# Expert weights loaded ahead of the stage, and token rows gathered in fp32 straight from x

## The chip, the cores and the metric

One core of a Trainium2 chip runs the whole program. The time is that of the device in microseconds (us), from one launch; the kernel before took 2052.31 us (median of 3 runs, 2049.75 to 2055.69). A core has five engines with queues of their own: TensorE (PE in the profile, with its weight loads as PEld), VectorE (DVE), ScalarE (ACT), GpSimd (POOL) and SyncE (SP), which here issues the DMAs. Between them stand semaphores, written out by hand in this kernel.

## The reference, cut to what matters

The program is a stack of layers on 256 tokens of 1024 numbers: a mixer, a mixture of experts, a gated embedding, a spatial gating mixer, an RWKV mixer and two FFNs. The change touches the mixture of experts and what stands before it:

```python
hn = _rmsnorm(x, g_ffn_norm)                   # [256, 1024]
logits = hn @ w_router + b_router              # 32 experts
top_vals, top_idx = lax.top_k(logits, 4)
gates = jax.nn.softmax(top_vals, axis=-1)
...
# for each expert e, for the tokens that chose it:
hgu = xb @ w_up_gate[e] + b_up_gate[e]         # 1024 -> 2048
x_glu = jnp.minimum(hgu[:, :1024], 7.0)
x_lin = jnp.clip(hgu[:, 1024:], -7.0, 7.0)
hact = x_glu * jax.nn.sigmoid(1.702 * x_glu) * (x_lin + 1.0)
ys = hact @ w_down[e] + b_down[e]              # 1024 -> 1024
# x + sum over the four experts of ys * gate
```

All weights are fp32. One expert has 8 MB of up and gate weights and 4 MB of down weights.

## The kernel before, in words

Seven stages follow each other (line 2828), with a barrier and a clearing of semaphores between them (`end_stage`, line 117). Two matter here.

**The mixer** (line 272). Its DMA queue on SP loads seven segments of `w_in` and two halves of `w_out` into the two buffers of `raw`, each as soon as the split of the segment before into high and low parts has left its buffer (lines 379 to 386). Its work buffers (`w_part`, `x_part`, `qkT`, `soft`, `positive`, `weight`, `rope`) lie beside each other. It ends with the projection by `w_out` on PE and four additions to x (line 891).

**The expert stage** (line 895), in two blocks with a barrier between them. The first block (line 969) has the router. SP issues nine small tables, then the first up load of expert 0, the up biases, and the other five loads of expert 0 into a ring of six buffers of 2 MB, four for up and two for down. DVE sums the squares of x and makes a diagonal of 1/rms; PE turns x by it (line 168), ACT and DVE copy it to `xT` with the norm's gain, and PE makes the logits (line 267, by the helper `matmuls`). Beside this ACT writes the scaled x in another order of columns (line 1036), and ACT and DVE split it into three bf16 `parts` (lines 1040, 1066, 1042, 1098). DVE then finds the top four, the gates and who was chosen; PE counts the rank of each token in its expert (lines 1009 to 1015); DVE and PE write a list of items, one for each expert and each further 64 tokens of it. Here there are 32 items.

The second block (line 1150) is the loop over items. Each item works on up to 64 tokens:

- `pick` (DVE, line 1279) marks in a 128x64 matrix which token goes to which slot, from `rank`; `gather` (PE, line 1180) multiplies the three bf16 parts by it, 48 pieces, into bank TURN; DVE multiplies by the gain into `xsT` (line 1284).
- 32 up matmuls of 512 columns (line 1214), in fp32 (the trace shows each fp32 matmul as two pieces), two buffer quarters at a time; each used buffer is released to SP through `up_used`. The biases come by four bf16 matmuls (line 1221) from `bias_part`, and the last of them releases the fourth buffer.
- The sum of the item before is added to x's four banks (line 1194), the slots' spread is turned (line 1230), the next item's `gather` runs, `act_h` is turned (line 1238, read with a step of four numbers), ACT copies it to `hT`, and 16 down matmuls follow (line 1250). They release `down_used`.

PE does this in this order, and SP reloads a buffer as soon as it is released, in the order up 0 to 3, down 0, down 1. POOL splits the biases into bf16 parts once (lines 1166 to 1176), beside the first item; PE waits for it before the first bias matmul.

The slots' gather in one place of code:

```python
1183  for k in range(KC):
1184      out = c.banks[:, TURN, k * CAP:(k + 1) * CAP]
1185      ins = matmuls(nc, out,
1186                    [parts[:, a, tc, k * P:(k + 1) * P] for tc in range(TC) for a in range(3)],
1187                    [pick[:, tc, :] for tc in range(TC) for a in range(3)])
```

## Time and profile before

| | us |
|---|---|
| median of 3 runs | 2052.31 |
| lowest and highest | 2049.75, 2055.69 |
| the profiled execution | 2056.73 |
| its span, first to last instruction | 2055.0 |
| PE busy in the span | 1804.6 (88%) |
| DVE, ACT, POOL busy | 770.2, 520.7, 212.3 |
| DMA's share of 16 engines | 66.6% |

The profile is of one execution. "Busy" counts the time in which an engine has an instruction in work; fp32 matmuls overlap, so PE's busy time is not time at its peak. In the timeline a row is a run of equal instructions: start in us from the span's start, busy us, engine, line, operation, out<-in, count, and in brackets how long the engine stood idle before and what released it. "PEclk" is the granted clock of TensorE, 1.00 at 2.4 GHz and 0.50 at 1.2 GHz; its mean over the span is 0.953.

### The profile page before, as it was taken

The page shows a single profiled execution, that of the slowest core. Times are in us where ns is not written, and L with a number is a line of the kernel's source. Part 1 is how long each engine was busy: PE and PEld are TensorE (multiplying, and loading weights), DVE is VectorE, ACT ScalarE, POOL GpSimd, SP SyncE. Part 2 cuts the span into 40 slices and gives each one's busy share as a digit, 9 for nine tenths or more (in the row PEclk, how much of TensorE's full clock was granted, in tenths as well). Part 3 has the DMA queues.
Part 4 walks back from the last instruction along what each step waited for, and adds up shares of the span by engine and source line. Part 5 has one row for each costly group of instructions (what it writes and reads, how often), then busy time and mean ns, then how long its engine had stood idle before and what let it go on. Part 6 is the DMA issues. An engine that isn't in the chain of part 4 may idle for free. (4 is left out here: it accounts for less than half of the span.)

```text
span 2055.0 us, 28922 instructions
## 1 busy us (share of the span) xinstructions
PE 1804.6 (88%) x11506; PEld 1113.2 (54%) x11506; DVE 770.2 (37%) x1364; ACT 520.7 (25%) x804; POOL 212.3 (10%) x149
## 2 busy tenths in 40 slices
PE   6887599998989898989988889798998998888997
PEld 5664233333333333333333368777997776847996
DVE  7923411111111111111111263836555647436555
ACT  4511111110111011101110235425442303215442
POOL 3511400000000000000000034320000103300000
PEclk9999799999999999999999989998999999988998
DMA  7312799999999999999999655329441431118530
GB/s 260 135 42 79 333 409 428 428 428 426 429 428 428 428 427 427 428 428 428 427 426 428 290 199 189 144 84 326 163 163 38 173 103 51 75 28 300 187 140 31
DMA packets 104399, 554.11 MB, mean 270 GB/s; under 512 B 17377, under 2 KB 27618, under 8 KB 78898
## 3 DMA queue, kind: packets, MB, share of 16 engines
q1 hardware_dynamic: 104338, 553.26, 66.6%
q8 instruction: 42, 0.69, 0.1%
q14 instruction: 19, 0.16, 0.0%
HBM read 551.15 MB, written 2.10 MB: 269 GB/s over the span
## 5 line engine op out<-in xcount | busy, mean ns | idle before, releaser
L1214 PE MATMUL banks<-ring,xsT 128*64 128x512 f32 x2048 | 458.0, 597 | 41.9 <-DMA ring<-in_w_up 41.0
L1214 PEld LDWEIGHTS banks<-ring,xsT 128*64 128x64 f32 x2048 | 143.2, 137 | 350.7 <-issue 266.5
L1313 DVE TENSOR_SCALAR glu<-banks 128x512 f32<-128x512 f32 x32 | 22.1, 692 | 663.2 <-PE banks L1221 663.2
L1250 PE MATMUL banks<-ring,hT 128*64 128x512 f32 x1024 | 230.2, 603 | 22.0 <-ACT hT L1269 22.0
L1858 PE MATMUL banks<-f_xT_hi,f_w_hi 128*128 128x256 f32 x512 | 146.7, 287 | 21.2 <-issue 21.2
L1250 PEld LDWEIGHTS banks<-ring,hT 128*64 128x64 f32 x1024 | 71.5, 138 | 158.6 <-issue 130.5
L1858 PE MATMUL banks<-f_xT_hi,f_w_lo 128*128 128x256 f32 x512 | 146.6, 286 | 0.0
L1858 PE MATMUL banks<-f_xT_lo,f_w_hi 128*128 128x256 f32 x512 | 146.6, 286 | 0.0
L1265 ACT ACTIVATE sig<-glu 128x512 f32<-128x512 f32 x32 | 20.1, 629 | 478.2 <-DVE glu L1313 478.2
L267 PE MATMUL banks<-w_arena 128*128 128x256 f32 (+1 forms) x400 | 120.1, 462 | 5.9 <-ACT w_arena L2649 3.6
L1858 PEld LDWEIGHTS banks<-f_xT_hi,f_w_hi 128*128 128x128 f32 x512 | 100.1, 195 | 24.4 <-issue 22.6
L1360 POOL TENSOR_TENSOR p_w_lo<-p_w_raw,p_w_hi 128x1024 fp32r<-128x1024 f32 x4 | 12.4, 3111 | 929.6 <-ACT p_w_hi L1404 929.5
L267 PEld LDWEIGHTS banks<-w_arena 128*128 128x128 f32 x400 | 77.5, 195 | 46.6 <-issue 32.3
L1858 PEld LDWEIGHTS banks<-f_xT_lo,f_w_hi 128*128 128x128 f32 x512 | 100.0, 195 | 1.8
L1858 PEld LDWEIGHTS banks<-f_xT_hi,f_w_lo 128*128 128x128 f32 x512 | 99.9, 195 | 0.0
L1943 DVE TENSOR_TENSOR f_w_lo<-ring,f_w_hi 128x1024 fp32r<-128x1024 f32 x64 | 78.2, 1224 | 28.8 <-ACT f_w_hi L1895 28.7
L1948 DVE TENSOR_TENSOR f_w_lo<-ring,f_w_hi 128x1024 fp32r<-128x1024 f32 x64 | 76.4, 1220 | 25.3 <-ACT f_w_hi L1900 25.3
L1868 PE MATMUL banks<-f_w_hi,f_h_hi 128*128 128x512 f32 x256 | 79.5, 392 | 0.0
L1868 PE MATMUL banks<-f_w_lo,f_h_hi 128*128 128x512 f32 x256 | 79.2, 390 | 0.0
L1868 PE MATMUL banks<-f_w_hi,f_h_lo 128*128 128x512 f32 x256 | 79.0, 390 | 0.0
L1271 ACT ACTIVATE e_y<-banks 128x512 f32<-128x512 f32 x32 | 19.1, 597 | 233.4 <-PE banks L1250 233.4
L1900 ACT ACTIVATE f_w_hi<-ring 128x1024 fp32r<-128x1024 f32 x64 | 66.8, 1052 | 31.6 <-PE banks L1868 23.2
(411 smaller groups left out, 2766.5 us busy)
## 6 DMA issues: line engine op xcount, KB each, us to landing
ring<-in_w_up SPq DMA_DIRECT2D x128, 2048.0 KB, 24.8
ring<-in_w_down SPq DMA_DIRECT2D x64, 2048.0 KB, 20.4
ring<-in_ffn_w SPq DMA_DIRECT2D x30, 2048.0 KB, 9.0
m_raw<-in_w_in SPq DMA_DIRECT2D x7, 2048.0 KB, 8.2
ring<-in_sgu_in SPq DMA_DIRECT2D x7, 2048.0 KB, 8.8
w_arena<-in_w_rkv SPq DMA_DIRECT2D x6, 2048.0 KB, 12.9
ring<-in_sgu_out SPq DMA_DIRECT2D x4, 2048.0 KB, 7.5
m_raw<-in_w_out SPq DMA_DIRECT2D x2, 2048.0 KB, 7.8
```

The costliest lines, as they stand in the source:

```text
L267: ins = nc.tensor.matmul(out, lhs[i], rhs[i], start=start and i == 0, stop=stop and i == n - 1)
L1214: ins = nc.tensor.matmul(c.banks[CAP * h:CAP * (h + 1), bank, :], xsT[:, k, :], up_slot[k // 2][:, o:o + BANK], start=k == 0, stop=False)
L1250: ins = nc.tensor.matmul(c.banks[CAP * h:CAP * (h + 1), DOWN, :], hT[:, at:at + CAP], down_slot[half][:, o:o + BANK], start=k == 0, stop=k ...
L1265: nc.scalar.activation(sig[:, :], glu[:, :], ACT.Sigmoid, scale=ALPHA).then_inc(sig_ready, 1)
L1271: nc.scalar.activation(y[:, :], c.banks[:, DOWN, :], ACT.Copy).then_inc(y_ready, 1)
L1313: v.tensor_scalar(glu[:, :], c.banks[:, GLU, :], LIMIT, None, ALU.min).then_inc(glu_ready, 1)
L1360: vec.tensor_tensor(w_part[1][:, k, :], w_raw[:, k, :], w_part[0][:, k, :], ALU.subtract).then_inc(w_low[k % 2], 1)
L1858: ins = nc.tensor.matmul(c.banks[:, j, 0:T], w[:, j, k, :], x[:, k, :], start=k == 0 and n == 0, stop=k == KC - 1 and n == 2)
L1868: ins = nc.tensor.matmul(c.banks[:, OUT + 2 * tc + o, :], h[:, j, tc * P:(tc + 1) * P], w[:, j, o * BANK:(o + 1) * BANK], start=False, sto ...
L1900: nc.scalar.activation(w2_hi[:, j, :], w2_raw[s][:, j, :], ACT.Copy).then_inc(w2_high, 1)
L1943: vec.tensor_tensor(w1_lo[:, j, :, :], w1_raw[s][:, :, j * P:(j + 1) * P], w1_hi[:, j, :, :], ALU.subtract).then_inc(w1_low, 1)
L1948: vec.tensor_tensor(w2_lo[:, j, :], w2_raw[s][:, j, :], w2_hi[:, j, :], ALU.subtract).then_inc(w2_low, 1)
```

## The change

Six buffers `front` of 2 MB take the place of the ring and are opened before the mixer's other buffers. The mixer's `w_part` and `x_part` lie at the same addresses (buffers 0 to 2), and `qkT`, `soft`, `positive` and `rope` are views of buffers 3 to 5; `weight` shares the memory of `scored`. At the end of the mixer's DMA queue SP loads the expert stage's nine tables, then expert 0's six loads, each after a wait for the last use of the mixer's data there. The expert stage becomes one block. The router works on x turned without a scale; the norm's gain is multiplied into `w_router` by POOL, and 1/rms comes in at the logits. The bf16 `parts` are gone: `gather` reads x itself in fp32, with a step of eight numbers, and `pick` holds 1/rms instead of 1. Ranks count from 1. Item 0 stands ahead of the loop; the list is finished and the gates are turned between its up matmuls, and the four opening matmuls of the sums come after its bias matmuls. POOL's bias split waits for `xs_ready`. At the end each of the four sums signals by itself. In the diff, the new `load_expert_tables` issues the tables as lines 972 to 982 did, and new DVE code for top four and gates, with the same operations on both halves of the tokens at once, is left out.

```diff
+UPS, DOWNS, SLOT = 4, 2, 4096
+FRONT = UPS + DOWNS
+UP_SLOT, DOWN_SLOT = (5, 4, 0, 1), (2, 3)
+LIST = 192
...
+        self.front = sb("front", [P, FRONT * SLOT])
...
+    def slot(self, i):
+        return self.front[:, i * SLOT:(i + 1) * SLOT]
+    def load_up(self, sp, e, q):
+        sp.dma_start(self.slot(UP_SLOT[q]), self.dram["w_up"][bass.ds(e * P, P), q * SLOT:(q + 1) * SLOT]).then_inc(
+            self.up_in[q], 16)
+    def load_down(self, sp, e, h):
+        sp.dma_start(self.slot(DOWN_SLOT[h]), self.dram["w_down"][bass.ds(e * (2 * P) + h * P, P), :]).then_inc(
+            self.down_in[h], 16)
...
+    with ExitStack() as under:
+        w_part = [under.enter_context(nc.sbuf_tensor(f"m_w_{n}", [P, KC, BANK], F32R)) for n in ("hi", "lo")]
+        x_part = [under.enter_context(nc.sbuf_tensor(f"m_x_{n}", [P, KC, T], F32R)) for n in ("hi", "lo")]
+    c.open_experts()
...
-        qkT = sb("qkT", [P, 4, PAIRS, T])
+        qkT = c.slot(3).rearrange("p (a i t) -> p a i t", a=4, i=PAIRS)
         decay = sb("decay", [P, HEADS, DIAG])
-        soft = sb("soft", [P, HEADS, DIAG])
-        positive = sb("positive", [P, HEADS, DIAG])
-        weight = sb("weight", [P, 2, 2, DIAG])
-        rope = sb("rope", [P, 4, TC, HEADS, HD // 2])
+        soft, positive = (c.slot(i)[:, 0:HEADS * DIAG].rearrange("p (h n) -> p h n", h=HEADS) for i in (4, 5))
+        rope = [c.slot(4 + i // 2)[:, HEADS * DIAG + i % 2 * BANK:HEADS * DIAG + (i % 2 + 1) * BANK].rearrange(
+            "p (c h d) -> p c h d", c=TC, h=HEADS) for i in range(4)]
...
+        weight = scored
...
+                c.load_expert_tables(sp)
+                sp.wait_ge(soft_done, PAIRS)
+                sp.wait_ge(roped, 2)
+                c.load_up(sp, 0, 0)
+                sp.wait_ge(arg_done, PAIRS)
+                c.load_up(sp, 0, 1)
+                sp.wait_ge(w_used, SEGS * KC)
+                c.load_up(sp, 0, 2)
+                c.load_up(sp, 0, 3)
+                c.load_down(sp, 0, 0)
+                sp.wait_ge(s_done, PAIRS)
+                c.load_down(sp, 0, 1)
...
-                for tc in range(TC):
-                    nc.scalar.activation(xn[:, tc, :].rearrange("t (k p) -> t k p", k=KC),
-                                         c.x[:, tc, :].rearrange("t (p k) -> t k p", k=KC), ACT.Copy,
-                                         scale=c.stat[:, tc:tc + 1]).then_inc(xn_ready, 1)
-                act.wait_ge(xn_ready, TC)
-                nc.scalar.activation(parts[:, 0, :, :], xn[:, :, :], ACT.Copy).then_inc(split_act, 1)
-                act.wait_ge(split_dve, 1)
-                nc.scalar.activation(parts[:, 1, :, :], xn[:, :, :], ACT.Copy).then_inc(split_act, 1)
...
+                def item(i, e):
                     for q in range(UPS):
                         sp.wait_ge(up_used, i * UPS + (q + 1 - UPS))
-                        load_up(sp, e, q)
+                        c.load_up(sp, e, q)
                     for h in range(DOWNS):
                         sp.wait_ge(down_used, i * DOWNS + (h + 1 - DOWNS))
-                        load_down(sp, e, h)
+                        c.load_down(sp, e, h)
+                sp.dma_start(chooser[:, :], c.dram["chooser"]).then_inc(bias_in, 16)
+                for i in range(3):
+                    sp.dma_start(bias[i * E:(i + 1) * E, :], c.dram["b_up"]).then_inc(bias_in, 16)
+                item(1, 1)
+                items = count(sp)
+                with sp.Fori(2, items) as i:
+                    item(i, listed_at(sp, i + EXPERT_AT, E - 1))
...
+                pool.wait_ge(c.router_in, 32)
+                nc.gpsimd.tensor_tensor(c.w_router[:, :, :], c.w_router[:, :, :],
+                                        c.col("g_ffn", 0, KC).unsqueeze(2).to_broadcast([P, KC, E]),
+                                        ALU.mult).then_inc(router_gained, 1)
+                pool.drain()
+                nc.gpsimd.memset(ones[:, :], 1.0).then_inc(ones_done, 1)
+                pool.drain()
+                for lo in (E, CAP + E):
+                    nc.gpsimd.memset(y[lo:lo + E, :], 0.0)
+                    pool.drain()
+                    nc.gpsimd.memset(spreadT[lo:lo + E, :], 0.0)
+                    pool.drain()
+                nc.gpsimd.memset(nothing[:, :], 0.0).then_inc(cleared, 1)
+                pool.drain()
                 pool.wait_ge(bias_in, 64)
+                pool.wait_ge(xs_ready, 1)
...
-                        ins = matmuls(nc, out,
-                                      [parts[:, a, tc, k * P:(k + 1) * P] for tc in range(TC) for a in range(3)],
-                                      [pick[:, tc, :] for tc in range(TC) for a in range(3)])
+                        ins = matmuls(nc, out, [c.x[:, tc, k:D:KC] for tc in range(TC)],
+                                      [pick[:, tc, :] for tc in range(TC)])
...
+                            if stop:
+                                ins.then_inc(summed, 1)
...
+                def open_sums():
+                    pe.wait_ge(cleared, 1)
+                    pe.wait_ge(list_done, 1)
+                    pe.wait_ge(gates_taken, 1)
+                    for i in range(2 * TC):
+                        nc.tensor.matmul(c.banks[:, SUM + i, :], nothing[:, 0:P], nothing[:, :], start=True, stop=False)
+                    pe.wait_ge(c.b_down_in, 32)
...
+                        if first and k == 3:
+                            finish_list()
+                        if first and k == 5:
+                            turn_gates()
...
+                    if first:
+                        open_sums()
...
+                for k in range(KC):
+                    for tc in range(TC):
+                        at = (k % 2) * T + tc * P
+                        ins = nc.tensor.transpose(c.banks[:, TURN_X + k // 2, at:at + P], c.x[:, tc, k * P:(k + 1) * P],
+                                                  c.ident[:, :])
+                    if k % 2:
+                        ins.then_inc(turned, 1)
+                pe.wait_ge(router_gained, 1)
+                for k in range(KC):
+                    pe.wait_ge(by_act, k // 2 + 1)
+                    for tc in range(TC):
+                        ins = nc.tensor.matmul(c.banks[:, LOGIT, tc * E:(tc + 1) * E], c.xT[:, k, tc * P:(tc + 1) * P],
+                                               c.w_router[:, k, :], start=k == 0 and tc == 0, stop=k == KC - 1,
+                                               skip_group_check=True)
+                ins.then_inc(routed, 1)
+                pe.wait_ge(c.r_const_in, 64)
+                pe.wait_ge(ones_done, 1)
+                pe.wait_ge(marked, 1)
+                for tc in range(TC):
+                    out = c.banks[:, RANK, tc * E:(tc + 1) * E]
+                    if tc:
+                        nc.tensor.matmul(out, ones[:, :], chosen[:, 0, 0, :], start=True, stop=False)
+                    ins = nc.tensor.matmul(out, c.upto[:, :], chosen[:, tc, 0, :], start=not tc, stop=True)
+                ins.then_inc(ranked, 1)
+                for tc in range(TC):
+                    ins = nc.tensor.matmul(c.banks[0:E3, EXTRA, 0:1], chosen[:, tc, :, :].rearrange("p b e -> p (b e)"),
+                                           ones[:, 0:1], start=tc == 0, stop=tc == 1)
+                ins.then_inc(ranked, 1)
+                gather(0)
+                pe.wait_ge(flagged, 1)
+                nc.tensor.matmul(c.banks[0:E3, EXTRA, 1:2], c.upto[0:E3, 0:E3], flag[:, :], start=True,
+                                 stop=True).then_inc(placed, 1)
+                item(0, True)
+                items = count(pe)
+                with pe.Fori(1, items) as i:
+                    item(i, False)
...
+                nc.scalar.activation(squares[:, 1, :], c.x[:, 1, :], ACT.Square, accum_out=c.stat[:, 1:2]).then_inc(
+                    squared, 1)
+                for b in range(KC // 2):
+                    act.wait_ge(turned, b + 1)
+                    nc.scalar.activation(c.xT[:, 2 * b:2 * b + 2, :].rearrange("p k t -> p (k t)"),
+                                         c.banks[:, TURN_X + b, :], ACT.Copy).then_inc(by_act, 1)
+                act.wait_ge(negated, 1)
+                for tc in range(TC):
+                    nc.scalar.activation(gate[:, tc, :], top[:, tc, 0:TOPK], ACT.Exp, bias=neg_max[:, tc:tc + 1],
+                                         accum_out=gate_sum[:, tc:tc + 1]).then_inc(exped, 1)
+                act.wait_ge(gates_taken, 1)
...
-                                              rank[:, tc, bass.ds(e, 1)], None, ALU.is_equal)
+                                              rank[:, tc, bass.ds(e, 1)], rstd[:, tc:tc + 1], ALU.is_equal,
+                                              ALU.mult)
...
+                v.nop().then_inc(halves_read, 1)
+                chain(dve, v.tensor_tensor_reduce(squares[:, 0, :], c.x[:, 0, :], c.x[:, 0, :], 1.0, 0.0, ALU.mult,
+                                                  ALU.add, c.stat[:, 0:1]))
+                dve.wait_ge(squared, 1)
+                c.dve_rstd(dve, v.tensor_scalar(rstd, rstd, 1.0 / D, EPS, ALU.mult, ALU.add), rstd)
+                dve.wait_ge(c.router_in, 32)
+                dve.wait_ge(c.r_const_in, 64)
+                dve.wait_ge(routed, 1)
...
+                dve.wait_ge(ranked, 1)
+                chain(dve, v.tensor_tensor(rank[:, :, :], c.banks[:, RANK, 0:TC * E].rearrange("p (c e) -> p c e", c=TC),
+                                           chosen[:, :, 0, :], ALU.mult))
+                pick_item(0, 0)
+                dve.wait_ge(ranked, 2)
+                v.tensor_tensor(flag[:, :], c.banks[0:E3, EXTRA, 0:1], c.extra_col[0:E3, 0:1], ALU.is_gt).then_inc(
+                    flagged, 1)
+                dve.wait_ge(bias_in, 64)
+                choose_item(0)
+                dve.wait_ge(gathered, 1)
+                take_gathered()
...
+                item(0, 0, 0, (1, 0), True)
...
+                        dve.wait_ge(summed, 2 * tc + h + 1)
```

## Rows read from the trace of the kernel before

**Rows 1.** The page's slices: GB/s in 40 equal parts of the span.

```profile
GB/s 260 135 42 79 333 409 428 428 428 426 429 428 428 428 427 427 428 428 428 427 426 428 290 199 189 144 84 326 163 163 38 173 103 51 75 28 300 187 140 31
```

**Rows 2.** Windows, mid-loop: PE, PEld, DVE, ACT, POOL busy; PEclk; DMA share; GB/s.

```profile
400.00:1000.00 600.00, 535.02 (x3296) 200.58 (x3294) 89.67 (x200) 71.49 (x102) 0.00 (x0) 1.00 1.01 428
```

**Rows 3.** Timeline, PE, items 1 and 2: start, us, operation, [idle before].

```profile
263.44 13.90 PE L1214 MATMUL banks<-ring,xsT 128*64 128x512 f32 x64
...
279.91 1.56 PE L267 MATMUL banks<-pick,parts 128*128 128x64 bf16 x48
282.35 0.72 PE L1238 MATMUL banks<-ident,act_h 128*128 128x128 f32 x4 [0.88 <-DVE xsT L1284]
283.75 7.09 PE L1250 MATMUL banks<-ring,hT 128*64 128x512 f32 x32 [0.69 <-ACT hT L1269]
290.67 13.90 PE L1214 MATMUL banks<-ring,xsT 128*64 128x512 f32 x64
```

**Rows 4.** Timeline, DVE, late in the loop: `glu` of two items.

```profile
1120.40 0.69 DVE L1313 TENSOR_SCALAR glu<-banks 128x512 f32<-128x512 f32 x1 [21.41 <-PE banks L1221]
...
1149.82 0.69 DVE L1313 TENSOR_SCALAR glu<-banks 128x512 f32<-128x512 f32 x1 [21.36 <-PE banks L1221]
```

**Rows 5.** Timeline, end of the mixer, head of the expert stage.

```profile
153.29 0.39 PE L396 MATMUL banks<-m_w_lo,m_x_hi 128*128 128x512 f32 x1
...
165.31 0.60 ACT L726 ACTIVATE xT<-banks 128x512 f32<-128x512 f32 x1 [9.05 <-PE banks L546]
...
189.88 1.23 DVE L153 CUSTOM_DVE_ANT_0 e_xn<-x 128x1024 f32<-128x1024 f32 x1 [1.15 <-PEq L120]
...
194.03 0.36 SPq L964 DMA_DIRECT2D ring<-in_w_up  x1
...
202.29 3.73 PE L267 MATMUL banks<-w_router_sb,xT 128*128 128x32 f32 x32 [1.02 <-issue]
...
210.10 0.18 DVE L1075 FIND_INDEX8 top_i<-top,logits 128x8 uint32<-128x32 f32 x1
```

**Rows 6.** Timeline, item 0: up matmuls, bias split on POOL, bias matmuls.

```profile
225.12 1.88 POOL L1166 CAST bias_part<-bias 32x2048 bf16<-32x2048 f32 x1 [32.37 <-POOLq L969]
...
232.69 16.25 PE L1214 MATMUL banks<-ring,xsT 128*64 128x512 f32 x64 [0.87 <-DVE xsT L1284]
...
247.86 1.88 POOL L1174 CAST bias_part<-bias 32x2048 bf16<-32x2048 f32 x1
...
249.93 0.62 PE L1221 MATMUL banks<-bias_part,choose 96*64 96x512 bf16 x4 [1.00 <-POOLq L1175]
```

**Rows 7.** Timeline, last item and end of the stage.

```profile
1162.88 0.60 ACT L1271 ACTIVATE e_y<-banks 128x512 f32<-128x512 f32 x1 [7.19 <-PE banks L1250]
...
1163.53 1.99 PE L1194 MATMUL banks<-e_y,spreadT 64*128 64x512 f32 x8 [0.70 <-ACT e_y L1271]
...
1165.57 2.48 DVE L1329 TENSOR_TENSOR x<-x,banks 128x512 f32<-128x512 f32 x4 [11.38 <-PE banks L1194]
```

**Rows 8.** Single lines: ns min/median/max, first and last start.

```profile
L407 PEld LDWEIGHTS banks<-ident,m_qk x16: 138/140/143, 57.5 to 59.2; 128*128 128x128 f32 x16
L1238 PEld LDWEIGHTS banks<-ident,act_h x128: 195/213/223, 255.1 to 1154.7; 128*128 128x128 f32 x128
L1238 PE MATMUL banks<-ident,act_h x128: 285/286/359, 255.1 to 1154.8; 128*128 128x128 f32 x128
L267 PE MATMUL banks<-w_router_sb,xT x32: 268/276/276, 202.3 to 205.7; 128*128 128x32 f32 x32
L1036 ACT ACTIVATE e_xn<-x,stat x2: 2149/2150/2150, 201.2 to 203.2; 128x1024 f32<-128x1024 f32 x2
L1404 ACT ACTIVATE p_w_hi<-p_w_raw x8: 1042/1050/1063, 1177.1 to 1185.7; 128x1024 fp32r<-128x1024 f32 x8
```

**Rows 9.** Timeline and windows: a clock drop; the clock after the router.

```profile
626.20 8.78 PE L1250 MATMUL banks<-ring,hT 128*64 128x512 f32 x32 [0.69 <-ACT hT L1269]
...
206.60:210.00 3.40, 0.00 (x0) 0.00 (x0) 2.62 (x4) 1.04 (x2) 0.00 (x0) 0.50 0.97 405
```

More of the change, by code:

```diff
@@ L1290, in choose_item, with item @@
                         chosen_ready, 1)
[L1292 to L1302 removed]
+                def item(i, e, b, after, first):
+                    if not first:
+                        dve.wait_ge(spread_turned, i)
                     for tc in range(TC):
@@ new lines, in _ @@
+                v.nop().then_inc(list_done, 1)
+                dve.wait_ge(gates_turned, 1)
+                for lo in (0, CAP):
+                    ins = v.tensor_copy(spreadT[lo:lo + E, :], c.banks[lo:lo + E, GATES, 0:T])
+                ins.then_inc(gates_taken, 1)
+                dve.wait_ge(gates_ready, 1)
+                item(0, 0, 0, (1, 0), True)
+                items = count(dve)
+                with dve.Fori(1, items) as i:
+                    item(i, listed_at(dve, i + EXPERT_AT, E - 1), listed_at(dve, i + BLOCK_AT, BLOCKS - 1),
+                         (listed_at(dve, i + (EXPERT_AT + 1), E - 1), listed_at(dve, i + (BLOCK_AT + 1), BLOCKS - 1)),
+                         False)
```

350 lines of the change are left out of this document (131 added, 219 removed).

## The prediction

> **What bounds the kernel now.** I read the slices of the page first, then the expert stage in windows, then the order of time inside it. The slices show that DMA is the busiest thing for half of the span: sixteen slices in a row stand at about 428 GB/s [rows 1]. One window of 600 us in that stretch gives PE 535 us busy, a DMA share of 1.01 and 428 GB/s [rows 2]. So the item loop (32 items, 12.58 MB of weights each) runs at the rate of the loads: 12.58 MB at 428 GB/s are 29.4 us, and one `glu` follows the last by 1149.82 - 1120.40 = 29.42 us [rows 4]. But PE is close behind. Early in the loop, where the first experts' weights wait in the buffers already, one item takes 290.67 - 263.44 = 27.23 us, and PE waits for no load in it [rows 3]. The slack of PE is therefore 2.19 us an item, and the change spends from it. In that chain the gather (48 bf16 pieces, 1.56 us) stands alone: PE then waits for `xsT`, turns `act_h`, waits for `hT` and goes on with the down matmuls, so every us added to the gather is added to the item.
>
> **The loads of expert 0.** Before, the first is issued at 194.03, after the barrier [rows 5]. They move into the mixer, on SP behind the `w_out` loads and nine small table loads; the last waits there are for projection and retention matmuls, the last of which start shortly after 153.29, 36 us before the expert stage does [rows 5]. Six loads take 29.4 us of DMA. Nothing later in the mixer is issued on SP or waits for a DMA, so I cost them at nothing; the cover is the rest of the mixer and the router, and without it item 0 would wait for its up weights.
>
> **The head of the stage.** Before, the first up matmul starts at 232.69 [rows 6]. After, from 189.9: a sum of squares 1.23 us (ACT does the other half beside it), four copies of a bank at 0.60 us on ACT from 191.1 on, 32 router pieces at 0.11 us beside them (3.73 us before), done about 195.5 (the turn of x before them, and POOL's product of the router's weights with the gain, lie beside the squares);  some twelve small DVE operations at about 0.2 us with their chain waits [rows 5], 2.8 us, to 198.3; the rank matmuls and `pick` 1.6 us, to 199.9; the gather 4.6 us (below) and `xsT` 0.69 us: 205.3. The four loads of biases, now first on SP, have 10 us to land. The split of x, the second block's barrier, the reading of the list and the gates are off this way. PE starts item 0 some 27 us earlier.
>
> **What is late next: the bias split on POOL.** It takes from 225.12 to 249.9 before, 24.8 us, and PE already waits 1.00 us for it [rows 6]. The change adds to it a wait for `xs_ready`, so it runs from 205.3 to 230.1. PE reaches the bias matmuls near 220 and stands for 10 us. Of the 27 us, 249.93 - 230.1 = 19.8 us are left. In the same wait stand the fourth up load of expert 1 (its buffer is released by the bias matmul), and behind it on SP both down loads. Then the rest of item 0: 263.44 - 249.93 = 13.5 us before [rows 3, 6]; plus 3.1 us of gather, 0.6 us for the four opening matmuls that now stand here (of the size of the four bias matmuls, 0.62 us), 0.5 us for the count, and 1.7 us since PE comes out of a long wait at the lower clock [rows 9]. Item 0 ends at 249.5 where it ended at 263.44: a gain of 14.0 us.
>
> **The gather, 31 times more.** 48 bf16 pieces become 16 fp32 matmuls, two pieces each: 32 pieces, each with a load of 128x128 fp32 weights. Such a piece with few columns goes at the pace of its weight load: 32 router pieces start from 202.3 to 205.7, 0.111 us each [rows 8]. That is the lower bound, 3.55 us, 1.99 us more than now, if the load did not mind how x is read. But x is read with a step of eight numbers. The nearest row is the turn of `act_h`, read with a step of four: its weight loads take 213 ns where those of the mixer's turn, with contiguous reads, take 140 ns [rows 8], and its four pieces take 0.72 us, the last 0.286 us long, hence (0.72 - 0.286) / 3 = 0.145 us apart [rows 3, 8] against 0.11. The upper bound is what a step of eight costs on ACT: 2150 ns for the same read of x with this step, 1051 ns for an operation of that size without it [rows 8], a factor of 2.05, 0.227 us a piece, 7.3 us a gather. I take 0.145: a row of the same engine and closest in form. The gather is then 4.64 us, 3.08 us more, and PE's own chain 30.31 us: the loads (29.42) no longer set the pace.
> The Trainium skill ("SBUF — State Buffer", section "Door 1: The DMA port swizzle") has a rule that speaks against this read: SBUF has 16-byte lines, a step of four fp32 is free, and beyond it each access to a new line pays. The trace disagrees on the free part (213 against 140 ns at a step of four), and the page gives no price beyond it; were the read free, the sum would be that of the first rival.
>
> **The clock.** Twice in the loop the granted clock drops from 2.4 to 1.2 GHz just as the down matmuls start: they take 8.78 us instead of 7.09, a price of 1.69 us [rows 3, 9]. Before each drop stands the stretch of short pieces and waits, gather, `xsT`, turn, `hT`, 3.8 us of an item. After the router's small fp32 pieces the clock is at 0.50 as well, though PE had been busy until 0.6 us earlier [rows 5, 9]. The change makes this stretch 3 us longer and fills it with pieces like the router's. Drops become more frequent; bounds are 2 in 31 items and every item. I take one in four, 0.42 us an item, since a longer item may also pass without one. Before, both drops fell into the slack; now each costs in full.
> So 31 items take 31 x (30.31 + 0.42) = 952.6 us, against 1162.88 - 263.44 = 899.4 us [rows 3, 7]: 53.2 us lost.
>
> **The end of the stage.** `summed` now counts each of the four last sums, so the four additions (2.48 us) start after the first instead of after all (1.99 us) [rows 7]: 1.4 us gained. Rope, weight and turned heads in other buffers cost nothing: same operations, in an order that had no use for the old separate ones. `pick` with a second operation and in fp32 runs under the up matmuls.
>
> **The sum.** -14.0 + 53.2 - 1.4 = +37.8 us. The profiled execution took 2056.73 us (span 2055.0): it would be 2094.5. It is 4.4 us over the median of the runs, so by that median 2052.3 + 37.8 = 2090.
>
> **Rivals.** *Cheap gather, few drops* (faster). The place is the pace of one piece. At 0.111 us PE's chain is 29.22 us; with two drops, 31 items take 909.2 us, 9.8 us more than before. Item 0's gains are 16.2 us (two shorter gathers). -16.2 + 9.8 - 1.4 = -7.8 us: 2044.5. It stops being faster at a piece of 0.119 us, or at five more drops. For it: the contiguous loads. Against it: `act_h`, and the clock after the router. Chance 0.2, of which a third ends within 0.3% or just over (a few drops more).
> *Steps cost double* (much slower). ACT's factor holds on PE: chain 32.9 us, 31 items 1021 us without drops and 1073 us with one each; item 0's gain is down to 9 us. +111 to +163 us: 2163 to 2215. For it: x is the very tensor, with the very step. Against it: a factor on another engine. Chance 0.18.
> *Cheap pieces, a drop each item* comes to 30.91 us an item and 2093, nearly my forecast by another way; it belongs to it. So does a step price with a drop in each item, 32.0 us an item, 2130. The forecast's own range, from no drop to that, is 2080 to 2130: 0.56 together. The 0.06 left lies between 2050 and 2080.
> *The loads don't hide.* If the loads in the mixer slowed it or landed late, item 0 would start later, but the bias split would hide 10 us of it; this only moves the sum by a few us.
>
> **How the numbers follow.** Forecast 2090, the likeliest case. A range of 2040 to 2180 takes in the cheap gather below, and the forecast with its clock bounds above, and reaches into the doubled price; outside is most of that rival. 0.3% (6.2 us) is about what a measurement can tell here. Faster by more: the cheap case with few drops, 0.14. Within: 0.07. Slower: 0.79.
>
> **What would show it.** In the profile after: the gather's group with 32 pieces an item, and its mean distance (0.11, 0.145 or 0.22 us); the time between two `glu` of mid-loop (29.4, 30 to 32, or 33 and over); the GB/s there, which must fall below 428 if PE sets the pace; the granted clock in the loop, below 0.97 with drops; the wait of PE before the bias matmul of item 0, about 10 us with POOL as its releaser; the first up matmul at about 205. I am wrong if mid-loop still runs at 428 GB/s, if the split ends before PE needs it, or if the clock stays at 1.00 with a gather of 4 us.

## The result, and the profile after

The changed kernel takes 2263.66 us (median of 4 runs, 2261.49 to 2265.68), the kernel before on the same chip 2052.48 us (4 runs): a ratio of 1.1025, 95% interval 1.1011 to 1.1039. That is slower, as forecast, but by 211 us where the forecast said 38, and outside the range given (2040 to 2180). The profiled execution took 2261.49 us, its span 2259.8 us, 204.8 more than the span before.

The slices of the page after, granted clock and GB/s (against [rows 1]):

```profile
PEclk9998788988888898888889889899899999988999
...
GB/s 247 112 272 124 252 327 351 363 329 372 333 384 331 338 367 330 384 330 371 334 337 378 329 255 98 277 189 75 288 159 148 100 158 27 113 1 248 199 148 29
```

One long window in mid-loop, with its columns as in [rows 2]:

```profile
400.00:1000.00 600.00, 573.46 (x2450) 280.28 (x2446) 75.64 (x166) 37.41 (x68) 0.00 (x0) 0.86 0.85 355
```

The loads no longer set the pace: 355 GB/s and a DMA share of 0.85, where 428 and 1.01 stood. PE is busy for more of the time than before, yet it does fewer instructions (2450, was 3296), its weight loads take 280 us instead of 201, and its clock is at 0.86 on average, where it was at 1.00. Both terms on which the forecast put a small price are there to be seen.

Two items on PE's timeline (against [rows 3]):

```profile
628.98 1.99 PE L1106 MATMUL banks<-e_y,spreadT 64*128 64x512 f32 x8
630.90 0.44 PE L1166 MATMUL banks<-ident,spread 128*128 128x128 f32 x2
631.17 7.77 PE L321 MATMUL banks<-pick,x 128*128 128x64 f32 x32
639.82 1.10 PE L1174 MATMUL banks<-ident,act_h 128*128 128x128 f32 x4 [0.88 <-DVE xsT L1276]
641.60 8.56 PE L1186 MATMUL banks<-front,hT 128*64 128x512 f32 x32 [0.69 <-ACT hT L1239]
649.99 13.90 PE L1148 MATMUL banks<-front,xsT 128*64 128x512 f32 x64
...
676.88 9.68 PE L1186 MATMUL banks<-front,hT 128*64 128x512 f32 x32 [0.69 <-ACT hT L1239]
```

The gather takes 7.77 us (1.56 before); 32 pieces, so (7.77 - 0.40) / 31 = 0.238 us from one to the next, with 0.40 the length of the last. The turn of `act_h` takes 1.10 us (0.72) and the down matmuls 8.56 and 9.68 us in turn (7.09). Everything else in the item is as it was. Items follow each other after 35.99 us on average (the first `glu` starts at 230.07, the last at 1345.89), item 0's slower stretch included; in mid-loop it is 35.84.

When the clock falls, by windows of the gather's line alone (length, PE, PEld, PEclk, DMA share, GB/s):

```profile
631.30:634.30 3.00, 3.00 (x14) 3.00 (x14) 1.00 0.99 421
634.70:637.70 3.00, 3.00 (x14) 3.00 (x14) 0.50 1.01 431
```

It falls from 2.4 to 1.2 GHz inside the gather: in this item some 3.2 us after its start, in the next 5.5 us, and so on in turn (nine items in a row from 631 on). It comes back 13.4 and 15.6 us after the gather's start, in the down matmuls, so that each item has some 10 us at 1.2 GHz, and its mean clock is 0.86. The gather does not care: 14 pieces in 3 us at either clock, and the very first gather of the stage, all of it at 1.2 GHz, takes 7.89 us.

Item 0 and the end of the stage (against [rows 6, 7]):

```profile
204.07 7.15 PE L1148 MATMUL banks<-front,xsT 128*64 128x512 f32 x24 [0.56 <-DVE xsT L1276]
...
228.97 1.07 PE L1155 MATMUL banks<-bias_part,choose 96*64 96x512 bf16 x4 [8.07 <-POOLq L1088]
229.97 1.88 PE L1132 MATMUL banks<-nothing 1*128 1x512 bf16 x4
231.78 3.57 PE L1106 MATMUL banks<-e_y,spreadT 64*128 64x512 f32 x8
...
245.99 10.09 PE L1186 MATMUL banks<-front,hT 128*64 128x512 f32 x32 [0.69 <-ACT hT L1239]
255.91 13.90 PE L1148 MATMUL banks<-front,xsT 128*64 128x512 f32 x64
...
1367.01 0.60 ACT L1241 ACTIVATE e_y<-banks 128x512 f32<-128x512 f32 x1 [8.66 <-PE banks L1186]
...
1368.82 2.48 DVE L1388 TENSOR_TENSOR x<-x,banks 128x512 f32<-128x512 f32 x4 [12.35 <-PE banks L1106]
```

The balance of the spans: item 0 ends at 255.91 instead of 263.44 (-7.5); the other 31 items take 1367.01 - 255.91 = 1111.1 instead of 899.4 us (+211.7); from there to the next stage's first PE work -0.9; the stages behind, which were not changed, +1.6. Together +204.9. All of the loss is in the loop.

### The profile page after: what moved, and what is told of

Its sections match the earlier page's. It is cut to its first block and busy times, and to the rows that moved or that the text cites. A ratio compares the mean times of both kernels' runs of the same rounds, so it can differ in the third digit from the quotient of the medians.

```text
span 2259.8 us, 27682 instructions
## 1 busy us (share of the span) xinstructions
PE 2063.7 (91%) x10962; PEld 1327.7 (59%) x10962; DVE 768.2 (34%) x1333; ACT 474.5 (21%) x771; POOL 212.7 (9%) x150
## 5 line engine op out<-in xcount | busy, mean ns | idle before, releaser
L1148 PE MATMUL banks<-front,xsT 128*64 128x512 f32 x2048 | 447.1, 594 | 0.6 <-DVE xsT L1276 0.6
L1148 PEld LDWEIGHTS banks<-front,xsT 128*64 128x64 f32 x2048 | 144.0, 137 | 296.2 <-issue 295.5
L1186 PE MATMUL banks<-front,hT 128*64 128x512 f32 x1024 | 292.6, 737 | 22.0 <-ACT hT L1239 22.0
L321 PE MATMUL banks<-pick,x 128*128 128x64 f32 x1056 | 256.5, 419 | 0.3 <-DVE pick L1270 0.3
L321 PEld LDWEIGHTS banks<-pick,x 128*128 128x128 f32 x1056 | 253.7, 334 | 0.4 <-DVE pick L1270 0.4
L1186 PEld LDWEIGHTS banks<-front,hT 128*64 128x64 f32 x1024 | 85.5, 170 | 213.7 <-issue 178.9
L1276 DVE TENSOR_TENSOR xsT<-banks,cols 128x512 f32<-128x512 f32 x33 | 22.8, 692 | 234.8 <-PE banks L321 234.8
L1239 ACT ACTIVATE hT<-banks 128x512 f32<-128x512 f32 x32 | 19.1, 597 | 294.3 <-PE banks L1174 294.3
## 6 DMA issues: line engine op xcount, KB each, us to landing
w_arena<-in_w_rkv SPq DMA_DIRECT2D x6, 2048.0 KB, 12.9
```

What stands on the lines that cost most here:

```text
L321: ins = nc.tensor.matmul(out, lhs[i], rhs[i], start=start and i == 0, stop=stop and i == n - 1)
L1148: ins = nc.tensor.matmul(c.banks[CAP * h:CAP * (h + 1), bank, :], xsT[:, k, :], up_slot[k // 2][:, o:o + BANK], start=k == 0, stop=False)
L1186: ins = nc.tensor.matmul(c.banks[CAP * h:CAP * (h + 1), DOWN, :], hT[:, at:at + CAP], down_slot[half][:, o:o + BANK], start=k == 0, stop=k ...
L1239: nc.scalar.activation(hT[:, :], c.banks[:, TURN, :], ACT.Copy).then_inc(hT_ready, 1)
L1276: v.tensor_tensor(xsT[:, :, :], c.banks[:, TURN, :].rearrange("p (k s) -> p k s", k=KC), c.col("g_ffn_rows", 0, KC).unsqueeze(2).to_broadc ...
```

## The experiments

The theory after the result: (a) the read with a step of eight makes a piece about twice as dear, and (b) the longer, thinner stretch of PE makes the clock drop in every item. Rivals: fp32 pieces that are dear in themselves, and a price that comes from the other parts of the change.

**1. The same gather, contiguous.** It reads 128 neighbouring columns, so other numbers of x land in the slots; the work is otherwise the same.

```diff
-[c.x[:, tc, k:D:KC] for tc in range(TC)]
+[c.x[:, tc, k * P:(k + 1) * P] for tc in range(TC)]
```

> The changed kernel with the gather reading 128 neighbouring columns of x instead of every eighth (so other numbers land in the slots; same number of instructions). In the changed kernel a gather takes 7.77 us and an item 36.0 us. If the step of the read is the cause, a piece goes back to the router's 0.111 us, the gather takes 3.6 us and PE's own chain 29.25 us an item. If the clock still drops once in most items (theory: short fp32 pieces and waits before the down matmuls), an item takes 30.6 to 31 us, the loads do not set the pace, and the run ends near 2092 us (2085 to 2100). If the clock stays up (rival), an item takes 29.3 to 29.4 us and the run ends near 2045. If fp32 pieces with 64 columns are dear in themselves, whatever the step (second rival), it stays at 2255 to 2264.

Measured: 2099.24 us (ratio 1.0219, 1.0193 to 1.0244). PE's timeline in mid-loop:

```profile
607.58 3.68 PE L321 MATMUL banks<-pick,x 128*128 128x64 f32 x32
612.14 0.73 PE L1174 MATMUL banks<-ident,act_h 128*128 128x128 f32 x4 [0.87 <-DVE xsT L1276]
613.55 8.46 PE L1186 MATMUL banks<-front,hT 128*64 128x512 f32 x32 [0.69 <-ACT hT L1239]
```

The gather is down to 3.68 us, 0.110 us a piece, which was the forecast's lower bound. An item takes 30.72 us. So the step costs 164 us: 127 of them (31 x 4.09) are the pieces' own, the rest mostly that the clock is low for longer. The down matmuls are still at 8.46 us in mid-loop: clock drops stay, in every item. They come later, 5.2 us after the gather's start, when the gather is over.

**2. Eight steps side by side.** The eight groups of the gather read x with steps of 1, 2, 3, 4, 6, 8, 12 and 16, one line each (again with other numbers of x in the slots).

```diff
-ins = matmuls(nc, out, [c.x[:, tc, k:D:KC] ...
+if k == 0:
+    ins = nc.tensor.matmul(out, flat[:, 0:128], pick[:, tc, :], **on)
...
+if k == 5:
+    ins = nc.tensor.matmul(out, flat[:, 0:1024:8], pick[:, tc, :], **on)
```

> The changed kernel with the eight groups of the gather reading x with steps of 1, 2, 3, 4, 6, 8, 12 and 16 numbers (other numbers land in the slots). It measures a piece at each step, by line. If a read pays for each new line of 16 bytes, steps of 4 and more all cost the same 0.24 us, 1 costs 0.11, 2 and 3 lie between. If it pays for the distance up to 32 bytes (rival), 4 costs 0.14 to 0.16 as the turn of act_h suggests, 6 more, and 8, 12 and 16 the same 0.24. If single distances collide in the memory (third), 8 and 16 are dear and 6 and 12 less.

Measured: 2210.68 us (one run). One gather on the timeline; the lines stand in the order of the steps, 1 to 16, four pieces each:

```profile
614.18 0.56 PE L1102 MATMUL banks<-pick,x 128*128 128x64 f32 x4
614.57 0.63 PE L1104 MATMUL banks<-pick,x 128*128 128x64 f32 x4
615.04 0.86 PE L1106 MATMUL banks<-pick,x 128*128 128x64 f32 x4
615.74 1.09 PE L1108 MATMUL banks<-pick,x 128*128 128x64 f32 x4
616.67 1.05 PE L1110 MATMUL banks<-pick,x 128*128 128x64 f32 x4
617.55 1.11 PE L1112 MATMUL banks<-pick,x 128*128 128x64 f32 x4
618.51 1.23 PE L1114 MATMUL banks<-pick,x 128*128 128x64 f32 x4
619.58 1.08 PE L1116 MATMUL banks<-pick,x 128*128 128x64 f32 x4
```

From one group's start to the next, divided by four, a piece takes 0.10 us at a step of 1, 0.12 at 2, 0.175 at 3, 0.23 at 4, 0.22 at 6, 0.24 at 8 and 0.27 at 12. The weight loads themselves take 192, 197, 261, 330, 317, 334, 369 and 311 ns (medians, steps of 1 to 16). The price rises to a step of four and is nearly flat from there; of the three cases of the expectation this is the first. The Trainium skill ("SBUF — State Buffer", section "Door 1: The DMA port swizzle") has a step of four fp32 free and a price beyond it; for weight loads of fp32 matmuls the trace disagrees on the place, four already pays in full, and agrees that a step is paid for.

**3. The read made contiguous, with the right numbers.** ACT copies x once into another order, in fp32, beside the router; the gather reads the copy.

```diff
+nc.scalar.activation(x_rows[:, tc, :].rearrange("t (k p) -> t k p", k=KC),
+                     c.x[:, tc, :].rearrange("t (p k) -> t k p", k=KC), ACT.Copy)
...
-[c.x[:, tc, k:D:KC] for tc in range(TC)]
+[x_rows[:, tc, k * P:(k + 1) * P] for tc in range(TC)]
```

> The changed kernel with a copy of x in the order of the slots' rows (ACT, 2 operations of 2.15 us beside the router), from which the gather reads neighbouring columns in fp32. The same loop as in the run with neighbouring columns of x itself: 30.6 to 31 us an item and 2092 us with a clock drop in most items, 29.4 us and 2045 us without. The copy ends before the ranks are there, so the first up matmul should start at about 200 (204.1 in the changed kernel), not later.

Measured: 2101.78 us (2095.72 to 2102.61; ratio 1.0221, 1.0197 to 1.0246), 30.72 us an item. The copy itself (4.01 us on ACT) is hidden. The first up matmul came at 202.24 where about 200 was expected, since the stage's first gather ran at half clock (7.06 us). So did the second, in item 0, and it shows the other half of the mechanism. The timeline:

```profile
234.30 6.92 PE L321 MATMUL banks<-pick,x_rows 128*128 128x64 f32 x32
```

and the window of it (the granted clock is the third number from the end):

```profile
234.30:241.20 6.90, 6.90 (x33) 6.73 (x32) 0.00 (x0) 0.38 (x1) 0.00 (x0) 0.50 0.05 19
```

A contiguous gather takes 6.92 us at 1.2 GHz and 3.68 at 2.4; one with a step of eight takes 7.89 at 1.2 GHz and 7.77 with its first 3 to 5 us at 2.4. Contiguous pieces go by the clock; pieces with a step of eight don't.

**4. The rest of the change without the fp32 gather.** The three bf16 parts and the gather of before, inside the changed structure.

```diff
-[c.x[:, tc, k:D:KC] for tc in range(TC)], [pick[:, tc, :] for tc in range(TC)]
+[parts[:, a, tc, k * P:(k + 1) * P] for tc in range(TC) for a in range(3)],
+[pick[:, tc, :] for tc in range(TC) for a in range(3)]
```

> The changed kernel with the three bf16 parts and the bf16 gather of before; everything else of the change stays. PE's chain is 27.2 us again, so the loads set the pace at 29.4 us an item, as before the change. The parts come later than the ranks (first up matmul about 204, as in the changed kernel), the bias split on POOL still holds item 0, which ends about 245 (263.4 before, 255.9 in the changed kernel). If the gather is the whole loss and the rest of the change a gain, the run is 14 to 22 us faster than the kernel before: 2030 to 2038 us. Rival: the rest of the change costs as well, and it ends at 2052 or above.

Measured: 2048.71 us (10 runs, 2044.47 to 2054.41; before 2054.37 in 13 runs; ratio 0.997, 0.9956 to 0.9985). The rest of the change is worth some 6 us, and the gather costs 2263.7 - 2048.7 = 215 us. Expected was a gain of 14 to 22 us and an end of item 0 at about 245. In this trace it ends at 250.52, 12.9 us before the 263.44 of [rows 3], but 5.4 us of that stood there when the expert stage began (184.5 against 189.88), and the unchanged stages behind take 4.4 us longer again (890.3 against 885.9). What is left of item 0's gain is 7.5 us: PE waits 7.0 us for the parts before the first gather, a wait that the fp32 gather does not have, and after the wait for the bias split the work runs at half clock. The 5.4 us go with a clock drop in the mixer that the profile of before has and this one has not. They don't come from the change: run 11 below has the mixer of before too, and its expert stage starts at 183.41. The windows, first before, then this kernel:

```profile
41.00:48.00 7.00, 3.87 (x9) 3.10 (x10) 4.92 (x9) 0.87 (x3) 1.26 (x1) 0.63 0.45 147
48.00:55.00 7.00, 7.00 (x29) 5.68 (x29) 6.40 (x14) 3.23 (x5) 4.64 (x10) 0.88 0.74 281
```

```profile
41.00:48.00 7.00, 5.71 (x25) 4.71 (x26) 6.37 (x9) 3.00 (x5) 3.07 (x4) 1.00 0.56 187
48.00:55.00 7.00, 7.00 (x41) 6.02 (x40) 6.62 (x16) 3.88 (x7) 5.05 (x10) 1.00 0.50 195
```

In item 0, PE still waits for the bias split:

```profile
230.48 1.06 PE L1160 MATMUL banks<-bias_part,choose 96*64 96x512 bf16 x4 [6.97 <-POOLq L1092]
```

**5. PE kept busy in its waits.** On top of run 3, dense bf16 matmuls of 512 columns beside `xsT` (four) and beside `hT` (three), into a bank that the next up matmuls open afresh.

```diff
 gather(i + 1)
+pe.wait_ge(halves_read, i + 2)
+for _ in range(4):
+    nc.tensor.matmul(c.banks[:, GLU, :], bias_part[:, 0:P], bias_part[:, 0:BANK], start=True, stop=True)
...
 ins.then_inc(h_turned, 1)
+for _ in range(3):
+    nc.tensor.matmul(c.banks[:, GLU, :], bias_part[:, 0:P], bias_part[:, 0:BANK], start=True, stop=True)
```

> The kernel with the reordered fp32 copy and the contiguous gather (2101.8 us, 30.72 us an item, down matmuls 8.46 us instead of 7.09 at full clock), plus dense bf16 matmuls of 512 columns where PE stands idle: four (0.21 us each) after the gather, beside DVE's xsT (0.88 us of waiting), and three after the turn of act_h, beside ACT's hT (0.69 us). They write zeros' or bias numbers into a bank that the next up matmuls open afresh, so the output is unchanged. If the clock falls because PE's stretch of short pieces and waits is too thin, the down matmuls come back to 7.09 us, PE's chain to about 29.3 us, the loads take over at 29.42 us an item, and the whole is 2101.8 - 31 x 1.3 = 2061 us (2055 to 2070). If the idle stretches have nothing to do with the fall (the fp32 pieces of the gather alone do it), the drops stay in every item and it is 2102 to 2112 us.

Measured: 2052.98 us (10 runs, 2049.35 to 2060.46; ratio 0.9995, 0.9985 to 1.0006), 49 us less than run 3. Timeline of one item:

```profile
625.95 3.68 PE L321 MATMUL banks<-pick,x_rows 128*128 128x64 f32 x32
629.47 1.03 PE L1175 MATMUL banks<-bias_part 96*128 96x512 bf16 x4
630.51 0.73 PE L1179 MATMUL banks<-ident,act_h 128*128 128x128 f32 x4
631.08 0.81 PE L1183 MATMUL banks<-bias_part 96*128 96x512 bf16 x3
```

The mid-loop window:

```profile
400.00:1000.00 600.00, 599.03 (x3122) 256.27 (x3120) 90.31 (x200) 44.73 (x81) 0.00 (x0) 1.00 1.01 428
```

Work that computes nothing made run 3's kernel faster, 2 us more than the range said, and as fast as the kernel before. The clock stays at 1.00, an item takes 29.35 us, and the loads are back at 428 GB/s. So with a contiguous gather, filling the waits is enough to hold the clock; the drop costs 30.72 - 29.35 = 1.37 us an item there. The waits alone don't make it fall in every item: the kernel before has the same two and waits for loads besides, and its clock fell in two items of 31.

**6. A shorter bias split.** On top of run 4, POOL's nine operations on 32 partitions become six, the first two on all 96.

```diff
-nc.gpsimd.tensor_copy(bias_part[0:E, :], bias[0:E, :])
-for i in range(1, 3):
-    ... i times (copy, subtract), then copy, on partitions i * E to (i + 1) * E
+nc.gpsimd.tensor_copy(bias_part[:, :], bias[:, :])
+nc.gpsimd.tensor_tensor(bias[:, :], bias[:, :], bias_part[:, :], ALU.subtract)
+nc.gpsimd.tensor_copy(bias_part[E:2 * E, :], bias[E:2 * E, :])
+...   # the same three steps for the last E partitions
```

> The changed kernel with the bf16 gather (2048.7 us), and POOL's bias split written in six operations on up to 96 partitions instead of nine on 32: by the rows of POOL (1.9 us a cast, 4.07 us a subtraction, whatever the partitions) 1.9 + 4.07 + 1.9 + 1.9 + 4.07 + 1.9 = 15.7 us instead of 24.7. It then ends at about 221, before PE reaches the bias matmuls at 223.5, so the wait of 7.0 us there goes. If that wait delays the loads of expert 1 and with them the whole loop: 7 us less, 2041 to 2043 us. If the loads are held by something else in item 0 (the down buffers, which come free only when its down matmuls are over), the loop is late by that all the same and it is 2046 to 2049 us.

Measured: 2036.84 us (4 runs, 2035.50 to 2040.56; ratio 0.9921, 0.9901 to 0.9941). It beats both kernels, and run 4 by 12 us, more than the 7 expected. POOL's first operations, and PE's bias matmul without a wait:

```profile
206.98 1.89 POOL L1083 CAST bias_part<-bias 96x2048 bf16<-96x2048 f32 x1 [17.64 <-DVE xsT L1292]
209.01 4.08 POOL L1085 TENSOR_TENSOR bias<-bias,bias_part 96x2048 f32<-96x2048 f32 x1
...
224.36 0.60 PE L1162 MATMUL banks<-bias_part,choose 96*64 96x512 bf16 x4
```

Three times the partitions cost POOL nothing more (1.89 and 4.08 us). With the wait the half clock behind it goes as well: opening the sums takes 1.03 instead of 1.88 us, the sums 1.99 instead of 3.79, the down matmuls 7.09 instead of 8.79. Item 0 ends at 238.83, 11.7 us before run 4's 250.52: 6.1 us up to the bias matmuls (the wait of 7.0, in a stage that began 1.3 us later), 5.6 us of clock behind them. The forecast had reckoned the wait and not the clock.

**7. Expert 0 loaded late.** On top of run 6, its six loads go out at the start of the expert stage.

```diff
 # mixer, SP
 c.load_expert_tables(sp)
-c.load_up(sp, 0, 0) ... c.load_down(sp, 0, 1)
 # expert stage, SP, behind the biases
+for q in range(UPS):
+    c.load_up(sp, 0, q)
+for h in range(DOWNS):
+    c.load_down(sp, 0, h)
```

> The same as the run with the short bias split, but expert 0's six loads go out on SP at the start of the expert stage, behind the biases, not in the mixer. The last up load lands about 186 + 4 x 4.9 = 206 to 208 us, PE needs it 10 us later, and the down loads land by 218, needed at 238; from there on the loop's loads wait for buffers in the same places as before. If so, loading early is worth nothing here: within 3 us of the run it is compared with. If early loading is what made the head shorter, it is 10 to 30 us slower.

Measured: 2036.88 us (4 runs, 2033.77 to 2039.90), the same as run 6. From the stage's first PE work to the end of item 0 it is 53.19 us in both. Loading expert 0 in the mixer is worth nothing here. The loads before item 1 are ready either way; what starts the loop's loads is the first buffer that item 0 releases.

**8. Sixteen turns instead of four.** On top of run 4, the turns of `act_h` are done four times over.

```diff
-for j in range(KC // 2):
+for j in [j for _ in range(4) for j in range(KC // 2)]:
```

> The kernel with the bf16 gather, with the four turns of act_h (step of four fp32) done four times over in each item, 16 in a row instead of 4, the same results written again. In the forecast the pace of a piece with a step was taken from this group of four: 0.145 us. If that was low because the first loads of a group of four lie in the idle time before it, sixteen in a row go at 0.21 to 0.24 us each (as the gather with a step of four did in the run with many steps: 0.23), the group takes about 3.7 us and the whole is 2 to 3 us an item longer, 2100 to 2140 us. If a turn is simply cheaper than a piece of a matmul, they go at 0.145 us and the group takes 2.5 us, 2080 to 2095 us.

Measured: 2044.57 us (one run), within the noise of run 4. Both ranges of the expectation were missed: it added the longer group to the item in full, though PE's chain of 27.23 us had 2.19 us of slack. The loads still set the pace (428 GB/s and a clock of 1.00 from 400 to 1000). The group:

```profile
612.03 2.19 PE L1179 MATMUL banks<-ident,act_h 128*128 128x128 f32 x16 [0.87 <-DVE xsT L1290]
```

(2.19 - 0.286) / 15 = 0.127 us a turn, at the same step of four at which a matmul's piece takes 0.23 us. The guess that a short group behind a wait had hidden the price falls: a turn is cheaper than an fp32 matmul's piece with the same step. Contiguous turns stand in the changed kernel, where PE turns x for the router:

```profile
184.36 1.94 PE L1194 MATMUL banks<-ident,x 128*128 128x128 f32 x16 [1.83 <-PEq L174]
```

The last is 0.272 us long, so they go at (1.94 - 0.272) / 15 = 0.111 us. A step of four costs a turn 0.016 us and a matmul's piece some 0.13 us. Why they differ is open.

**9 and 10. The changed kernel, filled.** Run 9 has the fillings of run 5 in the changed kernel; run 10 also a dense matmul after every eight pieces of the gather.

```diff
 # run 10, in the item; then in gather
+pe.wait_ge(halves_read, i + 2)   # before the gather, not after it
+gather(i + 1, True)
...
+if dense and k % 2:
+    nc.tensor.matmul(c.banks[:, GLU, :], bias_part[:, 0:P], bias_part[:, 0:BANK], start=True, stop=True)
```

> The changed kernel itself (2263.7 us, 35.99 us an item) with the same dense matmuls as in the filled run, four beside xsT and three beside hT. There the clock falls some 3 us after the gather has started, before either wait. If the fall there comes from the long gather with its thin pieces, the fillings come too late to prevent it and run at half clock, 0.43 us each: 1.7 us beside a wait of 0.88 and 1.3 us beside one of 0.69, so +1.4 us an item at most, less what a clock that rises earlier gives back to the down matmuls: 35.5 to 37.4 us an item, 2250 to 2307 us. If the waits alone made the clock fall, it would stay at full speed, 33.4 us an item (35.99 less 2.2 us of slower down matmuls and 0.4 us of slower turns), 2183 us.

> As that, with a dense matmul of 512 columns also after every eight of the gather's 32 pieces (four more an item, 0.21 us each at full clock, beside which the next weight load can run or not). If PE's thin work in the gather makes the clock fall, this holds it up: 33.4 us plus at most 0.9 us, 33.4 to 34.3 us an item, 2183 to 2212 us; what is then left over the contiguous gather with filling (2053.0 us, 29.35 us an item) is the price of the step alone, 4.1 us an item. If so few dense pieces don't hold it, it is 36 to 38 us an item, 2264 to 2330 us.

Measured: 2235.5 us (two runs) and 2264.68 us (two runs). Run 9 was 14 us under its range. Its timeline:

```profile
654.62 7.77 PE L321 MATMUL banks<-pick,x 128*128 128x64 f32 x32
662.19 1.91 PE L1173 MATMUL banks<-bias_part 96*128 96x512 bf16 x4
663.89 1.06 PE L1177 MATMUL banks<-ident,act_h 128*128 128x128 f32 x4
664.75 1.48 PE L1181 MATMUL banks<-bias_part 96*128 96x512 bf16 x3
```

The clock still falls inside the gather, 3.3 to 4.9 us after its start, and the fillings behind it run at half clock. But it comes back earlier, 10.4 to 13.4 us after that start instead of 13.4 to 15.6, so the down matmuls (7.09 to 8.07 us, where 8.56 and 9.68 stood) win more than the fillings cost: 34.99 us an item in mid-loop instead of 35.84. Run 10 came out as the second case of its expectation: four dense pieces don't hold the clock. Nor do they delay its fall: it comes 3.3 and 4.5 us after the gather's start in turn (3.2 and 5.5 in the changed kernel). The gather with them is 0.8 us longer or more, and an item takes 35.84 us again. So the long gather is enough to lower the clock, and the waits are not needed for it. That its few columns are the reason is not shown.

**11. The gather alone.** The kernel before with the fp32 gather from x, nothing else of the change; `pick` carries the norm's factor. The bf16 parts are made and not read.

```diff
-pick = sb("pick", [P, TC, CAP], BF16)
+pick = sb("pick", [P, TC, CAP])
...
-rank[:, tc, bass.ds(e, 1)], None, ALU.is_equal)
+rank[:, tc, bass.ds(e, 1)], c.stat[:, tc:tc + 1], ALU.is_equal, ALU.mult)
```

> The kernel before with one part of the change alone: the gather reads x itself in fp32 with a step of eight, pick carries the norm's factor. The three bf16 parts are still made, as before, but nothing reads them. The change without this part was 2048.7 us, with it 2263.7 us, 215 us more. If the parts don't touch each other, it is the kernel before plus that: 2054 + 215 = 2269 us (2258 to 2275), and 36.0 us an item. If the early loads or item 0's place ahead of the loop made the gather's price larger in the changed kernel, it is below 2250 us.

Measured: 2276.7 us (two runs, 2274.37 and 2279.02; ratio 1.1081, 1.1044 to 1.1119), 222 us over the kernel before and 2 over the range expected, 35.83 us an item. The start of its expert stage, which run 4 above refers to:

```profile
183.41 1.23 DVE L153 CUSTOM_DVE_ANT_0 e_xn<-x 128x1024 f32<-128x1024 f32 x1 [1.15 <-PEq L120]
```

The gather brings its whole price without any other part; the rival that the rest of the change makes it dear falls.

## Why the prediction was wrong in size

**What was right.** The direction, and the mechanism step by step: the gather stands alone in PE's chain; with it PE sets the pace instead of the loads; the clock falls more often. The chain's form holds: 27.23 us [rows 3] plus 7.77 - 1.56 for the gather is 33.44 us, and the 2.40 us that are left of the measured 35.84 stand in the turn (0.38) and the down matmuls (2.03 on average). POOL's split was forecast to take 24.8 us and took 24.6, PE waited for it (8.07 us, forecast 10), and the end of the stage gained 0.9 us (forecast 1.4). The loads of expert 0 hid, as said.

**What was luck.** The first up matmul was forecast for 205.3 and came at 204.07. But the forecast counts from 189.9, and the profiled stage began at 184.5: the way there took 19.6 us, not 15.4, and 3.3 of the 4.2 us more are the stage's first gather (7.89 us for 4.6).

**The first step that failed is the piece's price.** "I take 0.145: a row of the same engine and closest in form." It was 0.238 us, and the gather 7.77 us instead of 4.64: 3.13 us an item, 31 x 3.13 = 97 us. The row was a turn's, not a matmul's, and run 8 shows that these differ at the same step (0.127 against 0.23). Run 2 shows too that the step was not the difference: four and eight cost the same in a matmul. The upper bound, ACT's factor of 2.05 for the very same read, gave 0.227 and 7.3 us. I had argued against it as "a factor on another engine"; it was nearly right, and the true price lay just above it.

**The second is the clock.** "I take one in four, 0.42 us an item." It was every item. 35.84 us an item ((1367.01 - 255.91) / 31) less 33.44 leaves 2.40 us for the clock: 1.98 us more than forecast, 61 us in the loop. The count makes 39 of the 61 (31 drops at 1.69 us would be 52 us, 13 were reckoned), the price of a drop the rest: 1.69 us was that of a drop that comes as the down matmuls start; here it comes inside the gather and stays for the turn of `act_h` and more of the down matmuls. With the contiguous gather it costs 1.37 us (runs 3 and 5).

**The third is smaller:** item 0. Its stretch took 71.4 us (184.5 to 255.9) instead of 59.6. Of the 11.8 us more, 4.2 lie before the first up matmul, as said, and 3.1 in the second gather. The forecast had item 0 run on at full clock behind the wait for the split, but for its down matmuls; the bias, opening and sum matmuls also ran at half clock (6.5 us where 3.2 were reckoned), and the turn and the down matmuls took 1.10 and 10.09 us where 0.72 and 8.8 were reckoned. In the profile 5.4 us came back through the earlier start of the stage, which was chance: run 11, with the mixer of before, has it too (183.41).

The rival *Steps cost double* had the mechanism and both prices nearly right, and 0.18 of the chance; its upper end, 2215, was still 49 us short, 38 of them in the loop, since it put the drop at 1.69 us and the piece at 0.227. The range left most of it out.

**What the rest of the change gave** is 5.7 us (run 4), not the 14 + 1.4 us of the sum. The forecast's 14 us came with a gather that needs no parts; with the parts, PE waits for them, and the half clock behind the bias split takes more. Run 6 gets 12 us of it by a shorter split.

## What to carry to other kernels

Before an operand is read in place to save a copy, ask what the read costs in the form in which it is used: here the pieces of an fp32 matmul whose weights have a step of four or more go at half the pace or less, in every item, while the copy (4 us on an idle engine) is paid once. An upper bound taken from the same tensor with the same step on another engine deserves as much weight as a row of the same engine with another operation.

Where PE's own chain is close to the bound (27.2 of 29.4 us here), a longer stretch of small pieces costs twice: by its length (3.13 us an item more than reckoned here), and by the clock at which the work behind it runs (2.40 us). Where a wait can't be removed, dense work that computes nothing can pay for itself (49 us in run 5, 28 in run 9), but not always: in run 10 more of it gave the gain back.

## What the runs showed of the hardware

- Pieces of fp32 matmuls with 128x128 weights and 64 columns: 0.10 to 0.11 us with contiguous weights, 0.12 at a step of 2, 0.175 at 3, 0.22 to 0.24 at 4 to 8, 0.27 at 12. Turns of 128x128 take 0.111 us contiguous and 0.127 at a step of four.
- Contiguous pieces follow the clock (3.68 us a gather at 2.4 GHz, 6.92 at 1.2). Pieces with a step of eight don't (14 in 3 us at both; a whole gather at 1.2 GHz takes 7.89 us).
- Filling PE's waits of 0.88 and 0.69 us with matmuls of 512 columns kept the clock at 1.00 through the window of 600 us; the same item unfilled has a drop each time, at 0.94 on average. With the bf16 gather the same waits, unfilled, go with a drop in two items of 31, and behind the long gather the same filling did not hold it. The profile doesn't tell what the clock goes by.
- POOL takes 1.89 us for a cast of 2048 columns and 4.08 us for a subtraction, on 32 partitions and on 96.
